# First matmuls of the feed-forward layers with rounded input and remainder side by side as one 512-column operand

## The reference, cut to what matters

```
y = square(relu(h @ w1)) @ w2          # w1: 1024 x 4096, w2: 4096 x 1024
```

```
y = (silu(x @ w_gate) * (x @ w_up)) @ w2   # w_gate, w_up: 1024 x 2816, w2: 2816 x 1024
```

## Time and profile before

| | |
|---|---|
| median of 3 runs | 2379.93 us (2379.74 to 2381.53) |
| the profiled execution | 2379.12 us |
| its span | 2377.3 us |
| mean granted TensorE clock | 0.983 |
| TensorE busy | 2248.3 us, 95% |
| VectorE busy | 1582.5 us, 67% |
| ScalarE busy | 1134.3 us, 48% |

### The profile page before, as it was taken

One profiled execution on the slowest core, in us unless ns is written; L12 is line 12 of the kernel. 1 busy time (PEld: TensorE's weight loads), 2 busy tenths in 40 slices (PEclk: granted clock), 3 DMA queues, 4 the chain that ended last, 5 costly groups with the idle time before them and its releaser, 6 DMA issues.

```text
span 2377.3 us, 37368 instructions
## 1 busy us (share of the span) xinstructions
PE 2248.3 (95%) x15832; PEld 2076.3 (87%) x15832; DVE 1582.5 (67%) x1858; ACT 1134.3 (48%) x1519; POOL 380.3 (16%) x305
## 2 busy tenths in 40 slices
PE   4889999887999999999999999999999999999998
PEld 4778999875999899998799899999989979988997
DVE  6988986798655744689654675474466975457545
ACT  2344444785444534467633444353445665245432
POOL 2113223111200400300032140031012003303000
PEclk9899999998999999999999999999999999999999
DMA  9659884333555455755321455555566444124652
GB/s 347 227 166 328 309 305 135 95 95 102 197 193 193 169 188 182 176 159 141 107 89 37 141 184 189 183 171 196 188 142 190 145 109 124 52 75 158 215 182 102
DMA packets 302010, 397.35 MB, mean 167 GB/s; under 512 B 42976, under 2 KB 260698, under 8 KB 301845
## 3 DMA queue, kind: packets, MB, share of 16 engines
q1 hardware_dynamic: 283360, 336.75, 43.9%
q0 software_dynamic: 17504, 57.89, 7.7%
q10 hardware_dynamic: 980, 0.32, 0.1%
HBM read 393.86 MB, written 1.07 MB: 166 GB/s over the span
## 4 chain that ended last, share of the span: by engine, by line
PE 76%; DVE 14%; ACT 5%; issue 3%; DMA 1%; SPq 1%; POOL 0%; DVEq 0%; ACTq 0%; POOLq 0%
PE tiles L503 16%; PE tiles L504 15%; PE tiles L505 15%; PE y_rows L503 6%; PE y_rows L504 6%; PE y_rows L505 6%; PE tiles L897 6%; DVE weights_lo L1381 3%; ACT weights_hi L1006 2%; DVE ada_acc L1431 1%; DMA weights_raw<-in_attn_w_in_dram 1%; PE tiles L627 1%; ACT xt L1043 1%; DVE x_rows L1573 1%; DVE rnn_r L1710 1%
## 5 line engine op out<-in xcount | busy, mean ns | idle before, releaser
L1381 DVE TENSOR_TENSOR weights_lo<-weights_raw,weights_hi 128x2048 fp32r<-128x2048 f32 (+2 forms) x316 | 768.4, 2439 | 485.9 <-ACT weights_hi L1006 485.3
L503 PE MATMUL tiles<-xt_hi,weights_hi 128*128 128x256 f32 (+1 forms) x3216 | 918.6, 286 | 16.5 <-DVE xt_lo L1482 9.3
L504 PE MATMUL tiles<-xt_lo,weights_hi 128*128 128x256 f32 (+1 forms) x3216 | 912.3, 284 | 0.0
L505 PE MATMUL tiles<-xt_hi,weights_lo 128*128 128x256 f32 (+1 forms) x3216 | 912.3, 284 | 0.0
L1006 ACT ACTIVATE weights_hi<-weights_raw 128x2048 fp32r<-128x2048 f32 (+2 forms) x316 | 592.7, 1879 | 218.8 <-PE y_rows L505 170.1
L503 PEld LDWEIGHTS tiles<-xt_hi,weights_hi 128*128 128x128 f32 (+1 forms) x3216 | 612.0, 190 | 31.7 <-issue 23.8
L504 PEld LDWEIGHTS tiles<-xt_lo,weights_hi 128*128 128x128 f32 (+1 forms) x3216 | 612.1, 190 | 2.7
L505 PEld LDWEIGHTS tiles<-xt_hi,weights_lo 128*128 128x128 f32 (+1 forms) x3216 | 612.1, 190 | 0.0
L503 PE MATMUL y_rows<-weights_hi,hid_hi 128*128 128x512 f32 x608 | 239.4, 394 | 0.6 <-DVE weights_lo L1381 0.6
L504 PE MATMUL y_rows<-weights_lo,hid_hi 128*128 128x512 f32 x608 | 237.8, 391 | 0.0
L505 PE MATMUL y_rows<-weights_hi,hid_lo 128*128 128x512 f32 x608 | 237.2, 390 | 0.0
(11 more groups left out here) (351 smaller groups left out, 2936.5 us busy)
## 6 DMA issues: line engine op xcount, KB each, us to landing
weights_raw<-in_ffn_w_dram SPq DMA_DIRECT2D x132, 1024.0 KB, 5.0
weights_raw<-in_mlp_w_dram SPq DMA_DIRECT2D x64, 1024.0 KB, 6.2
weights_raw<-in_w_in_dram SPq DMA_DIRECT2D x52, 1024.0 KB, 5.2
ada_ring<-in_ada_w_dram POOLq DMA_DIRECT2D x76, 512.0 KB, 5.0
weights_raw<-in_rnn_w_in_dram SPq DMA_DIRECT2D x16, 768.0 KB, 4.7
weights_raw<-in_w_in_dram SPq DMA_DIRECT2D x32, 256.0 KB, 4.5
weights_raw<-in_w_branch_a_dram SPq DMA_DIRECT2D x32, 256.0 KB, 4.9
weights_raw<-in_w_branch_b_dram SPq DMA_DIRECT2D x8, 1024.0 KB, 5.0
```

What stands on the lines that cost most here:

```text
L503: pe.matmul(o, a, c, start=first, stop=False)
L504: pe.matmul(o, a, d, start=False, stop=False)
L505: return pe.matmul(o, b, c, start=False, stop=last)
L1381: dve.tensor_tensor(slot_view(WLO, m, NSPL), slot_view(RAW, m, NRAW), slot_view(WHI, m, NSPL).bitcast(F32), ALU.subtract).then_inc(*inc("l ...
```

## The change

`XH` and `XL` become the two halves of one tensor, at the addresses that they had. A new function `wide_slot` takes the place of `cols_slot` in the six feed-forward layers. Per group and chunk it issues one matmul of 512 columns, with the rounded weights as stationary operand and `XH` and `XL` side by side as moving operand, and one of 256 columns, with the weights' remainder and `XH`. Each group has a bank of its own: its first half holds hi*hi + lo*hi, its second half hi*lo. To empty it, ScalarE copies the second half to a new buffer `LB`, and VectorE adds it to the first half on its way to `RB` or `VB`. Relu and Silu then work in place on `RB`, and the product of the gated layers takes both factors from `RB` and `VB`.

```diff
-        XH = put("xt_hi", [P, KC, S], F32R, at=pos["at"])
         act1 = pos["at"]
-        pos["at"] += 8 * KB
-        XL = put("xt_lo", [P, KC, S], F32R)
+        XHL = put("xt_both", [P, 2, KC, S], F32R)
+        XH, XL = XHL[:, 0], XHL[:, 1]
...
+        LB = put("low_half", [P, 2, 2, S], at=hid_at + 54 * KB)
...
+            def wide_slot(label, ready=None):
+                n, wh, wl = open_slot(label)
+                banks = [topen(label + (0,), "D"), topen(label, "D")]
+                for j, k in [(j, k) for k in range(KC) for j in range(2)] if ready else [(j, k) for j in range(2) for k in range(KC)]:
+                    if ready:
+                        ready(k)
+                    m = slice(P * j, P * j + P)
+                    if k < KC - 1:
+                        pe.matmul(banks[j].rearrange("p (a b) -> p a b", a=2), wh[:, k, m], XHL[:, :, k, :], start=(k == 0), stop=False)
+                        pe.matmul(banks[j][:, 0:S], wl[:, k, m], XH[:, k, :], start=False, stop=False)
+                    else:
+                        pe.matmul(banks[j][:, 0:S], wl[:, k, m], XH[:, k, :], start=False, stop=False)
+                        ins = pe.matmul(banks[j].rearrange("p (a b) -> p a b", a=2), wh[:, k, m], XHL[:, :, k, :], start=False, stop=True)
+                        ins.then_inc(*inc("tile_done", label if j else label + (0,)))
...
-                        cols_slot((s, "w1", i), XH, XL, "A", ready=xready(s) if i == 0 else None)
+                        wide_slot((s, "w1", i), xready(s) if i == 0 else None)
...
-                        cols_slot((s, "g", i), XH, XL, "A", ready=xready(s) if i == 0 else None)
-                        cols_slot((s, "u", i), XH, XL, "D")
+                        wide_slot((s, "g", i), xready(s) if i == 0 else None)
+                        wide_slot((s, "u", i))
...
+            def low_half(s, name, i):
+                for j in range(2):
+                    key = (s, name, i) if j else (s, name, i, 0)
+                    bank = tile(key)
+                    if i:
+                        act.wait_ge(*past("free_D", (s, name, i - 1) if j else (s, name, i - 1, 0)))
+                    act.activation(LB[:, name == "u", j, :], bank[:, S:2 * S], ACT.Copy).then_inc(*inc("low_half", key))
...
-                        bank = tile((s, "w1", i))
-                        if i >= 2:
-                            act.wait_ge(*past("hid_ready", (s, i - 2)))
-                        evac((s, "w1", i), RB[:, i % 2, :], ACT.Relu, bank)
-                        act.wait_ge(*past("free_A", (s, "w1", i)))
+                        low_half(s, "w1", i)
+                        act.wait_ge(*past("free_D", (s, "w1", i)))
+                        act.activation(RB[:, i % 2, :], RB[:, i % 2, :], ACT.Relu).then_inc(*inc("hid_act", (s, i)))
+                        act.wait_ge(*past("hid_act", (s, i)))
                         hi_hidden(s, i, ACT.Square, RB)
...
-                        bank = tile((s, "g", i))
-                        if i >= 2:
-                            act.wait_ge(*past("hid_ready", (s, i - 2)))
-                        evac((s, "g", i), RB[:, i % 2, :], ACT.Silu, bank)
+                        low_half(s, "g", i)
+                        act.wait_ge(*past("free_D", (s, "g", i)))
+                        act.activation(RB[:, i % 2, :], RB[:, i % 2, :], ACT.Silu).then_inc(*inc("hid_act", (s, i)))
                         step((s, "u", i))
-                        act.wait_ge(*past("free_D", (s, "u", i)))
+                        low_half(s, "u", i)
+                        act.wait_ge(*past("hid_v", (s, i)))
                         hi_hidden(s, i, ACT.Copy, VB)
...
+            def both(label, dst):
+                for j in range(2):
+                    key = label if j else label + (0,)
+                    bank = tile(key)
+                    dve.wait_ge(*past("low_half", key))
+                    dve.tensor_tensor(dst[:, j * S:(j + 1) * S], bank[:, 0:S], LB[:, label[1] == "u", j, :], ALU.add).then_inc(*inc("free_D", key))
...
                         step((s, "w1", i))
-                        dve.wait_ge(*past("free_A", (s, "w1", i)))
+                        both((s, "w1", i), RB[:, i % 2, :])
+                        dve.wait_ge(*past("hid_act", (s, i)))
                         dve.tensor_tensor(VB[:, i % 2, :], RB[:, i % 2, :], RB[:, i % 2, :], ALU.mult).then_inc(*inc("hid_v", (s, i)))
...
                         step((s, "g", i))
+                        both((s, "g", i), RB[:, i % 2, :])
                         step((s, "u", i))
-                        bank = tile((s, "u", i))
-                        dve.wait_ge(*past("free_A", (s, "g", i)))
-                        dve.tensor_tensor(VB[:, i % 2, :], RB[:, i % 2, :], bank, ALU.mult).then_inc(*inc("free_D", (s, "u", i)))
+                        both((s, "u", i), VB[:, i % 2, :])
+                        dve.wait_ge(*past("free_D", (s, "u", i)))
+                        dve.wait_ge(*past("hid_act", (s, i)))
+                        dve.tensor_tensor(VB[:, i % 2, :], RB[:, i % 2, :], VB[:, i % 2, :], ALU.mult).then_inc(*inc("hid_v", (s, i)))
                         lo_hidden(s, i)
```

## The result

The changed kernel takes 2390.81 us (median of 4 runs, 2389.44 to 2391.32), the kernel before 2379.84 beside it (4 runs, 2379.16 to 2381.53): a ratio of 1.0045, 95% interval 1.0033 to 1.0057. It is slower by 11 us. The forecast was 2377.8, the range ended at 2390, so both missed; the rival "DVE sets sublayer 1 alone" had said 2389.3.

A forecast was written before the change was run, and what follows sets the result against it. PE was taken to bound the other feed-forward layers, level with DVE in sublayer 1. Gated layers -8.8, sublayer 3 -1.85 and sublayer 1 +8.5 gave -2.1 us: 2377.0 profiled, 2377.8 as median; range 2363 to 2390.

The forecast's parts named there:

- DVE sets sublayer 1 alone: Rival: in sublayer 1 every step pays its 1.46 us, 20 in place of 8.5, time 2389.3 us; chance 0.19.
- What bounds the kernel: PE bounds the other feed-forward layers; in sublayer 1 PE and DVE are level, DVE idle 18.9 of 174 us.
- the signs: After-trace, sublayer 1: DVE over 95% occupied or waiting for `hid_act`, PE waiting for `weights_lo` some 10 us.
- The merge saves 11.9 ns: On PE, one 512-column matmul costs 227.9 ns against 239.8 for two of 256; 1,920 merges save 22.8 us.
- The bounds (0 and 26.5): Per merged matmul on PE: at worst 239.8 ns, saving nothing; at best 213.3 ns, saving 26.5.
- The two pieces: The merged matmul's moving operand lies in two pieces 8 KB apart, which no row of the profile shows.
- Sublayer 1 +8.5: Sublayer 1 grows 8.5 us: 18.7 us of new DVE work less 10.8 of named waits, rounded up; bounds -2.5 and +20.
- The price of a step: Each DVE step of sublayer 1 grows by 1.46 us: two adds (0.76) and a wait for Relu.
- The tails and the starts: PE stalls 0.5 us in each of six tails, 1.5 per gated layer's start, and 0.7 in sublayer 3.
- the bank that I had at 0.8: At a gated layer's start, the second slot u waits 0.8 us for banks that DVE's adds empty late.

The follow-up runs named there:

- grouped: The changed kernel with each group's matmuls of one width kept together, except in the first slot of a layer: 2384.80 us, ratio 1.0015.
- experiment 2: The kernel before, with only sublayer 1 in the new form: 2390.63 us, ratio 1.0040.
- experiment 3: The changed kernel, with one modulation accumulation per step of sublayer 1 moved between DVE's adds and its wait for Relu: 2378.53 us, ratio 0.9993.

## Why the prediction was wrong

**What bounds the kernel: right.** PE bounds the other layers, and in sublayer 1 DVE and PE were level. PE's waits for splits there came to 8.7 us where I had some 10, and DVE was found waiting for `hid_act`, as I had it among the signs.

**"The merge saves 11.9 ns": the first step that failed.** It measured 7.5, so 14.4 us in place of 22.8, and 12.5 in place of 19.85 in the five layers that can use it: 7.4 us of the error, its largest part. I took both distances from runs of matmuls of one width, though the change makes them alternate, which the diff shows. For 227.9 in the new setting I offered that two forms of matmul last 394 ns alike; but a merged matmul lasts 390 to 400 ns too and still has its next start some 235 ns on, so durations could not show the distance. The bounds (0 and 26.5) did hold. The two pieces, which I named as the unknown, cost nothing. The Trainium skill (TensorE: Matmul & The Clock Gate, Back-to-back issue gap) gives some 2.5 ns beyond the columns for a warm isolated matmul, which is what a merge would save by it. The measured saving lies between that and my 11.9, and grouped it is 10, nearer to mine.

**"Sublayer 1 +8.5": the second step that failed, and the one that makes the change slower.** It measured +12.1. The price of a step was right: 1.46 predicted, and in the trace 0.75 of adds and 0.70 of waiting. Two things in what I made of it were wrong. I counted 15 steps in 180 to 354 us; DVE's products (L1640) show 14 there, and the layer has 16. And I let all 14.0 us of the named waits take up new work, 3.2 as Relu waits "already there" and 10.8 as slack. DVE's waits over the whole layer, 164.3 to 372.2 us before and 166.6 to 386.6 after (the first rows of each), show what they took:

```profile
DVE hid_val L1640 <- ACT hid_act L1010: 8.9, 5, 2.1
DVE x_rows L1552 <- PE y_rows L505: 3.1, 2, 2.6
```

```profile
DVE hid_val L1673 <- ACT hid_act L1140: 11.2, 16, 0.7
DVE weights_lo L1405 <- ACT weights_hi L1022: 2.5, 3, 1.3
```

With the others the sums are 19.1 and 19.2 us. The new work is 16 x 1.46 = 23.4. The old waits for Relu (8.9) went, and of the other 10.2 some 2.2 did, so 11.1 in all and not 14.0. 23.4 - 11.1 = 12.3, the 12.1 measured: DVE stands as idle as before, and the layer is longer by the adds. The rival said "the idle time moves instead of being filled", and DVE's 155.7 busy us of 174 against 155.1 before are that sentence in a row. Its 20 was too much; the old waits took about half. Nor did I price the clock, to which PE lost 5.8 us there and 1.5 before. The 12.1 is of one profile: by the 218.16 of experiment 2 it is 10.4.

**The tails and the starts: about right.** In the five other layers PE's 12.5 us came down to 2.5, so 10.0 went back where I had 9.2 (6.0 starts, 0.7, five tails of 0.5). The parts are of the kinds named. In sublayer 6, waits of PE from 1380 to 1575 us:

```profile
PE tiles L533 <- DVE weights_lo L1405: 0.9, 2, 0.6
...
PE tiles L533 <- DVE hid_val L1653: 0.5, 1, 0.5
```

The last is the bank that I had at 0.8, and the first was 0.4 before; the two rows between them (0.7 us for `x_rows`, 0.6 for `xt_both`) have the same values in the kernel before. A tail waits 0.4 rather than 0.5 in each of the five layers, and 1.7 in sublayer 1. So the new named waits are 1.4 us of the 2.3 that went back in this layer (352 merges at 7.5 ns less the 0.35 gained), and no named wait holds the other 0.9. In the lines by form, `low_half` takes 0.38 us, not 0.47:

```profile
L1126 ACT ACTIVATE low_half<-tiles 128x256 f32<-128x256 f32 x240 | 89.2, 378 | 255.0 <-PE tiles L537 254.6
...
L1653 DVE TENSOR_TENSOR hid_act<-tiles,low_half 128x256 f32<-128x256 f32 x152 | 61.4, 419 | 68.0 <-ACT low_half L1126 68.0
```

**The sum again:** the forecast's -2.1, +7.4 (merge), +3.6 (sublayer 1), +0.8 (starts and tails), +2.1 (sublayers 0, 2, 5 and 8, whose code is the same) = +11.8, the difference of the spans. Neither failed step alone puts the time outside the range (2390.81 less 7.4 or less 3.6 is inside); all the terms together do, by 0.8 us. That the rival's 2389.3 came so near is partly luck: its sublayer 1 was 8 us too long, and its merges in the other layers saved 7.4 too much.

**What stays open.** Why a matmul costs more after one of another width was not settled: the operand's pieces are excluded, the order is shown to matter, the cause is not. Nor is it settled how the 12.1 us divide between waits and the clock that falls after some of them; in experiment 3 most of both went together. The clock's part can be bounded. Between the changed kernel and experiment 2, with the same sublayer 1, PE's loss to the clock differs by 2.5 us and s1 by 1.7; between the two profiles of the kernel before, by 1.5 and 0.2. At 0.7 at most for each us lost, the 4.3 more than before are some 3 of the 12.1, as an estimate from these two pairs.

## What to carry to other kernels

Where an engine is nearly full, a new hand-over to another engine and back costs more than its instructions: each round is idle time of its own, and here about half of it lengthened the layer, until other work of the same engine was put into it. That took one moved instruction per step. When you set waits against new work, count only those that the new order can still use, count the steps in the trace, and allow for what PE's clock may lose after longer waits. Take a matmul's distance, not its duration, from rows in which its neighbours are those that it will have.

## What the runs showed of the hardware

- Matmuls of 512 and 256 columns, float32r at full clock, from start to next start: 227 to 230 ns and 120 ns when the next has the same width, about 235 and 117 when they alternate; the operand in one piece or two makes no difference.
- In the changed kernel's sublayer 1 the granted clock was 0.50 for some 6 us of full work behind the waits that end at 198.4 and 280.1 us (1.5 and 2.1 us). Before each of them PE had done 16 matmuls of one column in 1.8 us. Waits of 1.6 and 1.7 us that end at 189.3 and 265.0, behind matmuls of 512 columns, were not followed by a fall (1.00 in 189 to 195 and 262 to 276 us). In experiment 2 the wait of 1.8 us that ends at 189.4 was, so neither a wait's length nor its place alone tells.
- The same code of sublayer 0 lasted between 164.3 and 166.6 us over the 13 profiles.
